# Two changes to a decoder kernel: five of nine low weight parts per pair come from accumulating transfers, and the sums of the tokens move from GpSimd to VectorE

## The reference

```
h = rmsnorm(x, norm_g)
proj = h @ w_in                      # 1024 x 9232 weights
(rq, rk, rv, rz, dq, dk, dv, dz, db, da, gr, gd) = split(proj)
o_r = retention(rope(rq), rope(rk), rv)              # 4 heads
q, k, v = silu(causal_conv([dq, dk, dv]))            # 4 taps
o_d = gated_deltanet(l2norm(q), l2norm(k), v, ...)   # 8 heads, triangular solves, a recurrence
y = sigmoid(gr) * (o_r @ w_up_r) + sigmoid(gd) * (o_d @ w_up_d)
x = x + y @ w_o
```

## Time and profile before

| | |
|---|---|
| median of 3 runs | 2842.64 us |
| the profiled execution | 2846.34 us, span 2844.5 us |
| PE busy | 2629.5 us, 92% |
| VectorE busy | 1944.0 us, 68% |
| GpSimd busy | 1170.1 us, 41% |
| ScalarE busy | 842.4 us, 30% |
| DMA queues, share of 16 engines | 20.3% (SP), 6.0% (ScalarE) |

### The profile page before, as it was taken

How to read it: one execution, slowest core, us unless ns; L and a number is a source line. 1 busy time by engine, 2 the same in 40 slices (tenths; PEclk the granted TensorE clock), 3 DMA queues, 4 the chain that set the end, 5 groups by cost and what they waited for, 6 DMA issues and landing times.

```text
span 2844.5 us, 41656 instructions
## 1 busy us (share of the span) xinstructions
PE 2629.5 (92%) x14624; PEld 2193.1 (77%) x14624; DVE 1944.0 (68%) x4054; ACT 842.4 (30%) x1868; POOL 1170.1 (41%) x943
## 2 busy tenths in 40 slices
PE   7888988998889999999988889988988899999998
PEld 5677776777679989888866777776777789998887
DVE  8887878888865555534588788878878655554333
ACT  5334443434322212300133434343433122222001
POOL 5545444554421122434564445544544122224343
PEclk9999999999999999999999999999999999999999
DMA  4212221322231112333522212222221311124244
GB/s 163 83 50 72 61 80 47 85 60 65 60 90 38 45 47 69 112 100 111 162 80 71 80 45 79 61 65 60 71 77 49 90 43 40 39 67 132 93 130 152
DMA packets 296946, 222.07 MB, mean 78 GB/s; under 512 B 33218, under 2 KB 247572, under 8 KB 296484
## 3 DMA queue, kind: packets, MB, share of 16 engines
q1 hardware_dynamic: 264132, 162.22, 20.3%
q10 hardware_dynamic: 32608, 57.19, 6.0%
HBM read 178.40 MB, written 40.96 MB: 77 GB/s over the span
## 4 chain that ended last, share of the span: by engine, by line
PE 63%; DVE 21%; issue 5%; DMA 5%; SPq 3%; ACT 1%; POOL 1%; DVEq 0%; ACTq 0%
PE dense_ps L1014 10%; PE dense_ps L1016 10%; PE dense_ps L1018 10%; DVE arena L2616 5%; DMA w_raw<-in_w_in 4%; DVE arena L2619 3%; PE dense_ps L1216 3%; PE dense_ps L1218 3%; PE dense_ps L1217 3%; PE dense_ps L1038 2%; PE dense_ps L1039 2%; PE dense_ps L1040 2%; PE work L997 2%; SPq L844 2%; PE work L1218 2%
## 5 line engine op out<-in xcount | busy, mean ns | idle before, releaser
L1014 PE MATMUL dense_ps<-act_hi,w_hi 128*128 128x512 f32 x1208 | 487.5, 404 | 5.3 <-POOL w_lo L2915 2.4
L1016 PE MATMUL dense_ps<-act_lo,w_hi 128*128 128x512 f32 x1208 | 475.9, 394 | 0.0
L1018 PE MATMUL dense_ps<-act_hi,w_lo 128*128 128x512 f32 x1208 | 475.7, 394 | 0.0
L2915 POOL TENSOR_TENSOR w_lo<-w_raw,w_hi 128x1024 fp32r<-128x1024 f32 x80 | 203.3, 2541 | 468.2 <-DVE w_hi L2097 448.1
L3045 POOL TENSOR_TENSOR w_lo<-w_raw,w_hi 128x256 fp32r<-128x256 f32 x252 | 205.4, 816 | 394.6 <-ACT w_hi L1777 393.1
L1216 PE MATMUL dense_ps<-act_hi,w_hi 128*128 128x512 f32 x672 | 286.5, 426 | 0.0
L2279 DVE SCALAR_TENSOR_TENSOR arena<-arena,cols 128x512 f32<-128x512 f32 x288 | 279.3, 970 | 8.2
L1014 PEld LDWEIGHTS dense_ps<-act_hi,w_hi 128*128 128x128 f32 x1208 | 230.6, 191 | 54.9 <-issue 5.7
L1018 PEld LDWEIGHTS dense_ps<-act_hi,w_lo 128*128 128x128 f32 x1208 | 229.6, 190 | 50.0
L1218 PE MATMUL dense_ps<-act_hi,w_lo 128*128 128x512 f32 x672 | 264.3, 393 | 0.0
L1217 PE MATMUL dense_ps<-act_lo,w_hi 128*128 128x512 f32 x672 | 264.1, 393 | 0.0
(11 more groups left out here) (320 smaller groups left out, 6157.7 us busy)
## 6 DMA issues: line engine op xcount, KB each, us to landing
w_raw<-in_w_in SPq DMA_DIRECT2D x56, 512.0 KB, 3.8
w_raw<-in_w_in SPq DMA_DIRECT2D x84, 256.0 KB, 3.4
arena<-in_w_in SPq DMA_DIRECT2D x84, 256.0 KB, 2.9
arena<-l_scratch SPq DMA_DIRECT2D x64, 256.0 KB
arena<-gate_scratch ACTq DMA_DIRECT2D x64, 256.0 KB, 2.9
gate_scratch<-arena ACTq DMA_DIRECT2D x36, 256.0 KB, 2.8
w_raw<-in_w_out SPq DMA_DIRECT2D x18, 512.0 KB, 4.2
o_scratch<-arena ACTq DMA_DIRECT2D x32, 256.0 KB, 2.2
```

The source lines that it names most:

```text
L1014: eng.matmul(dense_ps[:, to, :], w_hi[:, slot, k, :], hi[:, k, seg], start=(k == 0), stop=False)
L1016: eng.matmul(dense_ps[:, to, :], w_hi[:, slot, k, :], lo[:, k, seg], start=False, stop=False)
L1018: mm = eng.matmul(dense_ps[:, to, :], w_lo[:, slot, k, :], hi[:, k, seg], start=False, stop=(k == KT - 1))
L2915: eng.tensor_tensor(w_lo[:, slot, :, :], w_from[second][:, :, :], w_hi[:, slot, :, :].bitcast(F32), ALU.subtract)\
```

## The change

Five of the nine parts, those that are plain weights (X11, X12, X22, J1, J2), are no longer subtracted by GpSimd. ScalarE writes the high part as before and then, in a second instruction, its negative into `w_lo`; GpSimd issues a transfer that adds the weights from device memory onto it. So `w_lo` becomes weight minus high part. PE waits for the transfer's semaphore. Two semaphores serve them, one for thin parts and one for J parts, and each transfer waits for the one before it on its semaphore. The four sums and the low parts of S1 to S4 stay with GpSimd.

SyncE may refill the weights' buffers once ScalarE has read them, not once GpSimd has. The places of the parts (`PART_AT`) move by one to three pieces to earlier ones. The fourteen `mix` steps go to VectorE unchanged, with new slots in the unit `first`. To free semaphores, the gates' and the tokens' loads at the layer's end share two, and the first two of the tokens' loads wait for the last of the gates'.

```diff
 PARTS = ("X11", "S1", "S2", "X12", "J1", "S3", "S4", "X22", "J2")
-PART_AT = (-14, -12, -9, -6, -3, 3, 5, 7, 10)
-PART_NO = {part: i + 1 for i, part in enumerate(PARTS)}
+PART_AT = (-14, -12, -9, -7, -5, 2, 4, 6, 7)
+ADDED_THIN, ADDED_WIDE = ("X11", "X12", "X22"), ("J1", "J2")
+ADDED = ADDED_THIN + ADDED_WIDE
+PART_NO = {part: i + 1 + len([p for p in PARTS[:i + 1] if p in ADDED]) for i, part in enumerate(PARTS)}
 THIN = {"X11": 0, "S1": 1, "S2": 2, "X12": 3, "S3": 4, "S4": 5, "X22": 6}
-LOWS = {step: i + 1 for i, step in enumerate(("sum_S1", "sum_S3", "X11", "sum_S2", "S1", "S2", "X12", "sum_S4", "J1", "S3",
-                                              "S4", "X22", "J2"))}
+LOWS = {step: i + 1 for i, step in enumerate(("sum_S1", "sum_S3", "sum_S2", "S1", "S2", "sum_S4", "S3", "S4"))}
...
-        for n in range(9):
-            at(6 + n, "mix", n)
-        for n in range(9, 13):
-            at(13 + n, "mix", n)
+        for n, slot in enumerate((8, 9, 10, 11, 12, 13, 14, 15, 15, 24, 26, 27, 30)):
...
+        def added(t, part):
+
+            if part in ADDED_THIN:
+                return thin_in, 16 * (len(ADDED_THIN) * t + ADDED_THIN.index(part) + 1)
+            return wide_in, 16 * (len(ADDED_WIDE) * t + ADDED_WIDE.index(part) + 1)
...
-                            eng.wait_ge(wp_lo.sem, wp_lo.after(t - 1, LOWS["X22"]))
+                            eng.wait_ge(wp_hi.sem, wp_hi.after(t - 1, PART_NO["X22"]))
+                            eng.wait_ge(wp_lo.sem, wp_lo.after(t - 1, LOWS["S4"]))
...
-                        eng.wait_ge(wp_lo.sem, wp_lo.after(t, LOWS["J1"]) if rest else wp_lo.after(t, 0))
+                        eng.wait_ge(wp_hi.sem, wp_hi.after(t, PART_NO["J1"] if rest else 0))
                         eng.dma_start(w_j, w_src(l, w_in, cols_of[rest])[:, CPH:KT, :]).then_inc(wj_in.sem, 16)
...
                         hi, lo = part_place(part, u, w_hi), part_place(part, u, w_lo)
-                        eng.wait_ge(wp_lo.sem, wp_lo.after(t, LOWS[part]))
+                        if part in ADDED:
+                            eng.wait_ge(*added(t, part))
+                        else:
+                            eng.wait_ge(wp_lo.sem, wp_lo.after(t, LOWS[part]))
...
-                            eng.wait_ge(wp_hi.sem, wp_hi.after(w, PART_NO[part] - 1))
+                            eng.wait_ge(wp_hi.sem, wp_hi.after(w, PART_NO[part] - 1 - int(part in ADDED)))
                             eng.activation(part_place(part, u, w_hi), part_from[part], ACT.Copy).then_inc(wp_hi.sem, 1)
+                            if part in ADDED:
+                                eng.wait_ge(wp_hi.sem, wp_hi.after(w, PART_NO[part] - 1))
+                                eng.activation(part_place(part, u, w_lo), part_from[part], ACT.Copy, scale=-1.0)\
+                                   .then_inc(wp_hi.sem, 1)
...
+                        elif what == "mix":
+                            mix(step[1])
...
-                            eng.tensor_tensor(part_place(part, u, w_lo), part_from[part], part_place(part, u, w_hi).bitcast(F32),
-                                              ALU.subtract).then_inc(wp_lo.sem, 1)
+                            if part in ADDED:
+                                tiles, block = {"X11": (low_k, 0), "X12": (high_k, 0), "X22": (high_k, 1),
+                                                "J1": (slice(CPH, KT), 0), "J2": (slice(CPH, KT), 1)}[part]
+                                done, count = added(w, part)
+                                if count > 16:
+                                    eng.wait_ge(done, count - 16)
+                                eng.dma_start(part_place(part, u, w_lo), w_src(l, w_in, pair_columns(u)[block])[:, tiles, :],
+                                              accum_op=ALU.add).then_inc(done, 16)
+                            else:
+                                eng.tensor_tensor(part_place(part, u, w_lo), part_from[part],
+                                                  part_place(part, u, w_hi).bitcast(F32), ALU.subtract).then_inc(wp_lo.sem, 1)
                             if part == "X11":
-                                eng.wait_ge(wp_lo.sem, wp_lo.after(w, LOWS["X11"]))
                                 eng.wait_ge(wp_lo.sem, wp_lo.after(w, LOWS["sum_S3"]))
                                 eng.tensor_tensor(raw_x["X11"], w_s, raw_x["X11"], ALU.subtract).then_inc(wp_lo.sem, 1)
                             elif part == "X12":
...
-                        elif what == "mix":
-                            mix(step[1])
```

More of the change, by code:

```diff
@@ L911, in _ @@
                     else:
-                        eng.wait_ge(wp_lo.sem, wp_lo.after(l * PAIRS + PAIRS - 1, LOWS["X22"]))
+                        eng.wait_ge(wp_hi.sem, wp_hi.after(l * PAIRS + PAIRS - 1, PART_NO["X22"]))
+                        eng.wait_ge(wp_lo.sem, wp_lo.after(l * PAIRS + PAIRS - 1, LOWS["S4"]))
                         load_w(n + BLK_HEADS, w_src(l, w_in, DZ0 + P + h * P))
@@ L1229, in pair_pieces @@
                             eng.wait_ge(dense_free[1].sem, dense_free[1].after(n + BLK_HEADS, 0))
-                            eng.wait_ge(wp_lo.sem, wp_lo.after(t, LOWS["X11"]))
+                            eng.wait_ge(*added(t, "X11"))
                             eng.matmul(b, part_place("X11", u, w_hi)[:, 0, :], act_hi[:, 0, early], start=True, stop=True)
@@ L3051, in delta_unit @@
                             elif part == "X12":
-                                eng.wait_ge(wp_lo.sem, wp_lo.after(w, LOWS["X12"]))
                                 eng.wait_ge(wp_lo.sem, wp_lo.after(w, LOWS["sum_S2"]))
                                 eng.tensor_tensor(raw_x["X12"], raw_x["X12"], raw_x["X11"], ALU.subtract).then_inc(wp_lo.sem, 1)
-                        elif what == "mix":
-                            mix(step[1])
                         elif what == "mask" and kind != "first":
```

94 lines of the change are left out of this document (49 added, 45 removed).

## The result

The changed kernel takes 2948.16 us (median of 3 runs, 2941.34 to 2949.43); the ratio to the kernel before is 1.0366, 95% interval 1.0339 to 1.0392. The prediction was 2794 us and a range up to 2852: wrong in its sign.

A forecast was written before the change was run, and what follows sets the result against it. PE was taken to wait mainly for VectorE, held while GpSimd computes. Terms -19.4 - 43.4 + 14 = -48.8 us against the profiled 2846.3 gave 2797.5, and 2794 us as median; range 2757 to 2852.

The forecast's parts named there:

- The mix steps: Moving mix to VectorE ends holds in each layer's unit first: -19.4 us, bounds -30 and -9.
- the holds: Beside solves and recurrences in the pairs, removing GpSimd's subtractions frees VectorE: 3.1 us per head, -43.4 us.
- (d) GpSimd writes the descriptors itself: Issuing transfers in the pairs: no row shows its time, bounds 0 and 816 ns, both 0 on PE.
- (c) The traffic grows: Extra reads lengthen the late load once per head: 1.0 us per head, +14 us (0 to 48).
- The places: Earlier places of parts in the pairs: 0.7 us gained for X12; J2's copies ahead of the tanh, charged 0.
- X12's slack: Between X12's high part and first use, the transfer has about 6.5 us, including 0.7 from the earlier place.
- J2's turn at ScalarE: J2's copies now stand ahead of the tanh: charged 0, or 25 us if ScalarE's waiting no longer covers them.
- The clock: Shorter stalls in first give back 2 us for each 4 us at the lower level; left in the range.
- Only `mix` pays: Rival: in the pairs holds give nothing, traffic costs little or nothing; 2823 us, chance 0.20.
- The slower rival: Transfers land late in the pairs, PE stands about 6 us per head: 84 us, 2878 us, chance 0.20.
- the largest term of the prediction: VectorE freed beside solves and recurrences in the pairs by removing GpSimd's subtractions: -43.4 us.

The follow-up runs named there:

- mix_only: Kernel before with only the mix steps moved to VectorE and their new slots, no transfers: 2823.5 us.
- moves_only: Kernel before with only the new places of the parts (PART_AT): 2888.7 us.
- after_long_rows: Changed kernel with the same five accumulating transfers and as many bytes, each as 128 rows of 1 or 2 KB: 2905.3 us.
- after_one_tile: Changed kernel with each accumulating transfer cut to its first tile, 128 rows of 512 bytes: 2882.7 us.
- plain_more_traffic: Changed kernel with overwriting transfers, plus a 256 KB transfer in SyncE's queue behind each load of a J part: 2870.0 us.

## Why the prediction was wrong

**The mix steps: right.** Forecast -19.4 us, measured -22. The convolution's steps in `first` take 862 ns, the gate 683, the scaling 476 and the mask 693 (compare), where I forecast them back at 748, 686, 464 and 686:

```profile
L2296 DVE SCALAR_TENSOR_TENSOR arena<-arena,cols 128x512 f32<-128x512 f32 x9 | 7.8, 862 | 0.1
...
L2310 DVE SCALAR_TENSOR_TENSOR arena<-arena 128x512 f32<-128x512 f32 x3 | 2.0, 683 | 0.0
L2293 DVE TENSOR_SCALAR arena<-arena,cols 128x512 f32<-128x512 f32 x4 | 1.9, 476 | 0.0
...
L2497 DVE TENSOR_TENSOR arena<-mk,arena 128x512 f32<-128x512 f32 x1 | 0.7, 693 | 0.0
```

**"That is -43.4 us" (the holds): the step that failed first.** I took away the subtractions and put nothing in their place, with 0 as the bound "if a transfer's issue holds VectorE as the subtraction did". In place of each stands an issue of 1.3 us on GpSimd, and behind it GpSimd runs on for up to 2.7 us while VectorE stands, where behind a subtraction the two took turns. It holds VectorE not as the subtraction did but longer, up to 2.65 us at once. The prediction had also put the holds on instructions with two inputs; the scaling that is held here has one beside its scalars. The bound was on the wrong side of nothing: VectorE's busy time, which was to fall by some 43 us below that of `mix_only`, rose by 20 (1922.6 to 1942.4). In the kernel's time accumulating costs 77 us over a transfer that overwrites, and one that overwrites gains nothing either (see below).

**"(d) GpSimd writes the descriptors itself ... both 0 on PE": the same error a second time.** I bounded the issue by 816 ns and costed it at nothing because GpSimd has free time. But GpSimd's time is paid by VectorE. I knew that from the earlier trace rows and used it only for what went. The Trainium skill, "SBUF — State Buffer", section "Who interferes with whom", has two statements that bear on this. For the writing of descriptors it names GpSimd as the one that is starved; of the ports that GpSimd shares with VectorE it says that whichever of the two starts first keeps them and the other blocks. The prediction drew on the first alone. The trace shows VectorE as the one that waits: a scaling kept for 2.65 us by an issue and the two instructions behind it.

**"(c) The traffic grows": place right, cause and size wrong.** The place was the one of the earlier trace rows; its price was not 1 us per head but 3.5 idle (74.3 - 25.2 over 14 heads) and more of clock behind it. Of the 49 us the new places alone make 15 (`moves_only`: 39.9). The rest came with the transfers, 14 of it with their bytes (73.7 to 59.5 from `after_long_rows` to `after_one_tile`); the same traffic at the J loads cost nothing (`plain_more_traffic`). All of it was paid because the copy stood behind the load.

**The places: not costed.** The prediction named them for X12's slack and for J2's turn at ScalarE, at 0. They cost 44 us alone.

**The clock: left in the range for `first`, not seen for the pairs.** Within the pairs of both layers, their ends left aside, the granted clock was at the lower level twice before (at 174 and at 2068 us), and after it is so in every head; in the head shown, twice, once behind each of the two places. It is 39.8 of the 101.8 us of span.

**The parts together.** From 2845: mix -22, places +44, copies +3.5, and 2870.7 for overwriting transfers, which is what these three already give; accumulating +77: 2948. That the sum closes is partly luck, since the places are worth 21 in the presence of accumulating transfers, and that leaves a zero for the holds under overwriting transfers which no run shows by itself: none has overwriting transfers at the old places.

**"Only `mix` pays"** named the mechanism, "the issue of a transfer holds it as long", and with it 2823 us. `mix_only` gave 2823.5 without any transfer; with transfers the holds were longer than that rival had them, and the places and the load came on top.

**The slower rival** had the right sign and 2878 us, by a wrong mechanism. PE's waits for late transfers are 15.7 us, with median landings of 3.7 and 5.5 us, inside the 6.5 us of slack that I had worked out.

**Open.** Why VectorE gets no turn behind an issue, and why an accumulating issue is 0.45 us longer and goes by the rows; and how the 43 us that the rows carry divide between GpSimd and the DMA engines, whose share for these transfers fell with them from 11.5% to 9.3% of the span, with PE's wait for late transfers from 15.7 to 4.5 us.

## What to carry to other kernels

Where an engine's work is moved off because it holds another, cost what stands in its place by the same mechanism: issuing a transfer from GpSimd is GpSimd work, and here a chain on VectorE paid for it, more than for the subtraction. Before buying bandwidth or taking work away, look at what stands queued behind the instruction that waits for a load; swapping two instructions of ScalarE was worth 46 us here, as much as the largest term of the prediction. And in a serial chain at a full TensorE, price a longer stall with the clock behind it: in `moves_only` that was more than half of the loss.

## What the runs showed of the hardware

- An accumulating transfer's issue on GpSimd took 1306 ns in the mean (256 or 512 rows of 512 bytes, the mean of both), 910 with 128 rows, of 512 bytes or of 1 and 2 KB; an overwriting one with 256 or 512 rows took 760. GpSimd's next instructions have longer rows behind an accumulating one (1188 ns for 751) that overlap it; they end 0.45 us later, all together.
- While GpSimd made a subtraction and its next two instructions (3.01 us), 4.6 instructions of VectorE started, and none took over 1.17 us. With an accumulating issue in place of the subtraction (2.66 us) 1.7 started, and one took up to 2.65 us; with an overwriting one (2.21 us) 1.3, and up to 2.19 us. Each is the mean of 42 pairs.
- Accumulating packets of 512 bytes kept the DMA engines for 69 ns each (11.5% of 16 times 2946 us over 78624 packets), overwriting ones for 48.
- A wait of 5 us of PE in the midst of the pairs was followed by a granted clock of 0.50 for the first 4 us of its work.
